# Two attention stages: the first pair's bias, queries and keys loaded in the stage ahead

## The reference

```python
# layer 0, attention part
s = einsum('bthd,bsd->bths', qib, ki) * (D_I ** -0.5)
score = einsum('bth,bths->bts', wb * (H_I ** -0.5), relu(s))
_, idx = top_k(where(adm, score, -inf), 256)
bias = t5_table[_t5_bucket(sel_pos - pb)]
logits = einsum('bthd,btkhd->bhtk', qb, ks) * (DH ** -0.5) + bias
out = einsum('bhtk,btkhd->bthd', softmax(logits), vs)
# layer 1, attention part
rel = clip(q_pos[:, None] - k_pos[None, :], -128, 128) + 128
logits = einsum('bthd,bshd->bhts', q, k) * (DH ** -0.5) + rel_table[rel]
out = einsum('bhts,bshd->bthd', softmax(logits), v)
```

## Time and profile before

| | us |
|---|---|
| median of 3 runs | 3113.55 |
| lowest and highest | 3110.88, 3113.63 |
| the profiled execution | 3111.68 |
| its span in the trace | 3109.8 |
| front stage ends, pa begins | about 580 |
| trunk 0 ends, pc begins | about 2006 |

### The profile page before, as it was taken

One profiled execution on the slowest core, in us unless ns is written; L12 is line 12 of the kernel. 1 busy time (PEld: TensorE's weight loads), 2 busy tenths in 40 slices (PEclk: granted clock), 3 DMA queues, 4 the chain that ended last, 5 costly groups with the idle time before them and its releaser, 6 DMA issues. The chain is left out here.

```text
span 3109.8 us, 60214 instructions
## 1 busy us (share of the span) xinstructions
PE 2917.9 (94%) x25097; PEld 2716.4 (87%) x25097; DVE 1653.1 (53%) x2959; ACT 951.2 (31%) x1984; POOL 1321.6 (42%) x1082
## 2 busy tenths in 40 slices
PE   7999999886789899999999999899889999999998
PEld 5859999664679899999999999766689999999998
DVE  6399999564646644445346400055536644444345
ACT  3341211354433433332101311165524333332001
POOL 2112212373533877776334222100114877775334
PEclk8999999998889999999999999999989999999999
DMA  5816763633241122223321232352121122224222
GB/s 211 256 61 228 235 212 106 180 108 110 99 164 55 49 83 83 82 70 133 102 83 62 81 103 74 95 191 86 64 85 45 66 83 80 71 78 153 83 74 72
DMA packets 160465, 338.82 MB, mean 109 GB/s; under 512 B 21033, under 2 KB 94529, under 8 KB 152193
## 3 DMA queue, kind: packets, MB, share of 16 engines
q1 hardware_dynamic: 119856, 281.64, 27.0%
q10 hardware_dynamic: 40336, 53.31, 4.8%
HBM read 268.30 MB, written 79.49 MB: 112 GB/s over the span
## 5 line engine op out<-in xcount | busy, mean ns | idle before, releaser
L108 PE MATMUL tr_acc<-tr_quad_hi,ah_ring_hi 128*128 128x264 f32 x2432 | 696.3, 286 | 18.8 <-DVE tr_kept L1142 13.2
L110 PE MATMUL tr_acc<-tr_quad_hi,ah_ring_lo 128*128 128x264 f32 x2432 | 694.7, 286 | 0.0
L109 PE MATMUL tr_acc<-tr_quad_lo,ah_ring_hi 128*128 128x264 f32 x2432 | 692.4, 285 | 0.0
L552 POOL TENSOR_TENSOR ah_ring_lo<-ah_raw,ah_ring_hi 128x512 fp32r<-128x512 f32 (+1 forms) x402 | 553.9, 1383 | 183.0 <-ACT ah_ring_hi L889 169.2
L108 PEld LDWEIGHTS tr_acc<-tr_quad_hi,ah_ring_hi 128*128 128x128 f32 x2432 | 461.0, 190 | 19.7 <-DVE tr_kept L1142 13.6
L109 PEld LDWEIGHTS tr_acc<-tr_quad_lo,ah_ring_hi 128*128 128x128 f32 x2432 | 461.2, 190 | 0.1
L110 PEld LDWEIGHTS tr_acc<-tr_quad_hi,ah_ring_lo 128*128 128x128 f32 x2432 | 460.4, 189 | 0.0
L550 POOL CAST ah_ring_hi<-ah_raw 128x512 fp32r<-128x512 f32 (+1 forms) x172 | 113.4, 659 | 592.3 <-PE tr_acc L110 527.2
L108 PE MATMUL tr_acc<-tr_part_hi,ah_ring_hi 128*128 128x352 f32 x1038 | 335.5, 323 | 2.0 <-DVE tr_kept L1191 2.0
L109 PE MATMUL tr_acc<-tr_part_lo,ah_ring_hi 128*128 128x352 f32 x1038 | 332.8, 321 | 0.0
L110 PE MATMUL tr_acc<-tr_part_hi,ah_ring_lo 128*128 128x352 f32 x1038 | 332.5, 320 | 0.0
(11 more groups left out here) (399 smaller groups left out, 6484.6 us busy)
## 6 DMA issues: line engine op xcount, KB each, us to landing
f_ada_w<-in_w_ada_dram SPq DMA_DIRECT2D x48, 1024.0 KB, 5.5
scratch_inner<-tr_kept ACTq DMA_DIRECT2D x88, 264.0 KB, 2.4
tr_staged<-scratch_inner SPq DMA_DIRECT2D x44, 528.0 KB, 4.0
ah_raw<-in_w_gate_dram SPq DMA_DIRECT2D x44, 512.0 KB, 3.5
ah_raw<-in_w_up_dram SPq DMA_DIRECT2D x44, 512.0 KB, 4.5
ah_raw<-in_w_down_dram SPq DMA_DIRECT2D x64, 256.0 KB, 3.1
f_raw<-in_w_dram SPq DMA_DIRECT2D x24, 512.0 KB, 7.4
out_z_dram<-f_stage ACTq DMA_DIRECT2D x60, 176.0 KB, 1.9
```

Source lines behind the costliest of these rows:

```text
L108: pe.matmul(out, w_hi, hi, start=start, stop=False)
L109: pe.matmul(out, w_hi, lo, start=False, stop=False)
L110: return pe.matmul(out, w_lo, hi, start=False, stop=stop)
L552: pool.tensor_tensor(lo[:, 0:width], own, hi[:, 0:width].bitcast(F32), ALU.subtract).then_inc(w_ready, 1)
```

## The change

For each attention stage three of the four loads of pair 0 (bias, queries, keys) are taken out of the stage and issued by SP at the end of the stage ahead, into memory that is dead there and that the attention stage keeps at the same address. The values of pair 0 are still loaded in the attention stage. A class `FirstPair` holds the three tiles and one semaphore. In the front stage SP now waits for the skewed tables, for the last split of the weights and for the stores of all projected chunks, issues the three loads, then stores the mask, then waits for the loads. In trunk 0 SP waits until the stores of the first five units of `z1` (30 of them, ten for each of three semaphores) have landed, issues the loads and waits for them. In the attention stage POOL and PE no longer wait for pair 0, and the counts of later pairs are one lower. Tiles of the attention stage are laid around the kept region, `spread` now ahead of `probT`, and the late sample values of pa take the kept region's place instead of the two bias buffers.

```diff
+            if ahead:
+                for r in range(3):
+                    sp.wait_ge(stored[r], 16 * 2 * 5)
+                ahead.loads(sp)
+                ahead.done(sp)
...
+        ahead = next_pair(m, raw_at)
+        assert ahead.end <= raw_at + 2 * 8 * KD * P
...
+            sp.wait_ge(lines_out, 48)
+            sp.wait_ge(w_ready, len(units))
+            projected = store_no[plan.last_step[len(units) - 3]] + 1
+            for r in range(3):
+                sp.wait_ge(stored[r], 16 * len(range(r, projected, 3)))
+            ahead.loads(sp)
             store_mask(sp)
-            sp.wait_ge(lines_out, 48)
+            ahead.done(sp)
...
+class FirstPair:
+    def __init__(self, m, name, z, q0, k0, skew, width, at):
+        nc = m.nc
+        self.at, self.end = at, at + 8 * width + 8 * T
+        self.bias = nc.alloc_sbuf_tensor_at(f"{name}_bias0", [P, 2, width], F32, offset=at)
+        self.q, self.k = (nc.alloc_sbuf_tensor_at(f"{name}_{x}0", [P, T], F32, offset=at + 8 * width + 4 * T * n)
+                          for n, x in enumerate("qk"))
+        self.sources = (z[q0][:, 0:T], z[k0][:, 0:T], shifted(skew[0:2], P, width + P - 1, P - 1, width))
+        self.landed = m.sem(f"{name}_first")
+    def loads(self, sp):
+        q, k, bias = self.sources
+        sp.dma_start(self.bias[:], bias).then_inc(self.landed, 16)
+        sp.dma_start(self.q[:], q).then_inc(self.landed, 16)
+        sp.dma_start(self.k[:], k).then_inc(self.landed, 16)
+    def done(self, sp):
+        sp.wait_ge(self.landed, 48)
...
-                sp.dma_start(q[b][:], z[q0 + g][:, 0:T]).then_inc(qk_in[b], 16)
-                sp.dma_start(k[b][:], z[k0 + g][:, 0:T]).then_inc(qk_in[b], 16)
+                if g:
+                    sp.dma_start(q[b][:], z[q0 + g][:, 0:T]).then_inc(qk_in[b], 16)
+                    sp.dma_start(k[b][:], z[k0 + g][:, 0:T]).then_inc(qk_in[b], 16)
...
+                if g:
+                    sp.dma_start(bias[b][:], shifted(skew[2 * g:2 * g + 2], P, width + P - 1, P - 1, width)).then_inc(bias_in[b], 16)
...
-                if i == 0:
-                    pool.wait_ge(bias_in[b], 16 * (g // 2 + 1))
+                if i == 0 and g:
+                    pool.wait_ge(bias_in[b], 16 * ((g + 1) // 2))
...
-                if i == 0:
-                    pe.wait_ge(qk_in[b], 32 * (g // 2 + 1))
+                if i == 0 and g:
+                    pe.wait_ge(qk_in[b], 32 * ((g + 1) // 2))
```

More of the change, by code:

```diff
@@ L8 @@
+import math
 from contextlib import ExitStack
@@ L295, in done, with trunk_phase @@
         pool.wait_ge(self.w_lo, AHEAD)
-def trunk_phase(nc, io, l, x, c, places, early):
+def trunk_phase(nc, io, l, x, c, places, early, next_pair=None):
     last = l == 1
@@ L379, in trunk_phase @@
         y_stored = m.sem(f"{name}_y_stored")
+        ahead = next_pair(m, base + 11 * QUAD) if next_pair else None
+        assert ahead is None or ahead.end <= base + 14 * QUAD
         block = m.block()
@@ L1522, in chunk, with front_phase @@
         return self.units[u][1][a] if kind == "z" else None
-def front_phase(nc, io, moving, low_at, score, c):
+def front_phase(nc, io, moving, low_at, score, c, next_pair):
     plan = FrontPlan()
@@ L1532, in front_phase @@
     with Tools(nc) as m:
+        raw_at = nc.sbuf_base
         raw = [m.sb(f"f_raw{b}", [P, 2 * KD * P]) for b in range(2)]
@@ L2065, in __init__, with attention_phase @@
         self.quads = [(lo, min(lo + 4, self.blocks)) for lo in range(0, self.blocks, 4)]
-def attention_phase(nc, name, io, z, q0, k0, vt, v0, skew, width, heads, back, mask, side, ident, mix, early=None, next_weights=None):
+class FirstPair:
[14 more added lines that the diff above has]
+        sp.wait_ge(self.landed, 48)
+def attention_phase(nc, name, io, z, q0, k0, vt, v0, skew, width, heads, back, mask, side, ident, mix, first, early=None, next_weights=None):
     pairs = heads // 2
@@ L2105, in attention_phase, with sb @@
     with Tools(nc) as m:
[L2106 to L2110, removed]
+        def sb(tile, shape):
+            if nc.sbuf_base <= first.at < nc.sbuf_base + 4 * math.prod(shape[1:]):
+                m.sb(f"{name}_kept_free", [P, (first.end - nc.sbuf_base) // 4])
+            return m.sb(tile, shape)
+        q, k = [first.q, sb(f"{name}_q1", [P, T])], [first.k, sb(f"{name}_k1", [P, T])]
+        v = [sb(f"{name}_v{b}", [P, TILES, P]) for b in range(2)]
+        bias = [first.bias, sb(f"{name}_bias1", [P, 2, width])]
+        extra_all = sb(f"{name}_extra", [P, 4, T]) if mask is not None else None
         extra = [extra_all[:, a, :] for a in range(4)] if mask is not None else None
-        prob_all = m.sb(f"{name}_prob", [P, 6 * max(keys)])
+        prob_all = sb(f"{name}_prob", [P, 6 * max(keys)])
         prob = [prob_all[:, max(keys) * a:max(keys) * a + max(keys)] for a in range(6)]
[L2114 to L2117, removed]
+        spread = [sb(f"{name}_spread{b}", [P, 4 * P]) for b in range(2)]
+        probT = [sb(f"{name}_probT{a}", [P, 2 * max(keys)]) for a in range(2)]
+        least, total, inv = (sb(f"{name}_{x}", [P, 2 * U]) for x in ("least", "sum", "inv"))
+        oT = [sb(f"{name}_oT{b}", [P, T]) for b in range(2)]
         dots = [m.ps(f"{name}_dots{a}", [P, 1024]) for a in range(2)]
@@ L2120, in attention_phase @@
         out = [m.ps(f"{name}_out{b}", [P, 512]) for b in range(2)]
-        s_q = m.sb(f"{name}_s_q", [P, G, 4, S])
-        s_k_new, s_v_new = m.sb(f"{name}_s_k_new", [P, 2 * G, S]), m.sb(f"{name}_s_v_new", [S, 256 * G])
+        s_q = sb(f"{name}_s_q", [P, G, 4, S])
+        s_k_new, s_v_new = sb(f"{name}_s_k_new", [P, 2 * G, S]), sb(f"{name}_s_v_new", [S, 256 * G])
         own_sides = G if mask is None else 1
-        s_k = [m.sb(f"{name}_s_k{g}", [P, 2, side.past]) for g in range(own_sides)]
-        s_v = [m.sb(f"{name}_s_v{g}", [P, side.blocks, 256]) for g in range(own_sides)]
+        s_k = [sb(f"{name}_s_k{g}", [P, 2, side.past]) for g in range(own_sides)]
+        s_v = [sb(f"{name}_s_v{g}", [P, side.blocks, 256]) for g in range(own_sides)]
         if mask is not None:
             s_k.append(extra_all[:].rearrange("p (c a) n -> p c (a n)", c=2))
-            s_v.append(bias_all[:].rearrange("p b h n -> p (b h n)").rearrange("p (i n) -> p i n", n=256))
-        s_bias = [m.sb(f"{name}_s_bias{g}", [P, side.keys]) for g in range(G)]
-        s_prob = [] if mask is None else [m.sb(f"{name}_s_prob", [P, side.keys])]
+            s_v.append(nc.alloc_sbuf_tensor_at(f"{name}_s_v{own_sides}", [P, side.blocks, 256], F32, offset=first.at))
+            assert first.end - first.at >= 4 * side.blocks * 256
+        s_bias = [sb(f"{name}_s_bias{g}", [P, side.keys]) for g in range(G)]
+        s_prob = [] if mask is None else [sb(f"{name}_s_prob", [P, side.keys])]
         s_prob += [prob_all[:, side.keys * b:side.keys * b + side.keys] for b in range(2 - len(s_prob))]
         s_mask = s_prob[0]
[L2133 to L2136, removed]
+        s_tail = [sb(f"{name}_s_tail{b}", [S, P]) for b in range(2)]
+        s_least, s_total, s_inv = sb(f"{name}_s_least", [P, G, 4]), sb(f"{name}_s_sum", [P, G]), sb(f"{name}_s_inv", [P, G])
+        s_o = [sb(f"{name}_s_o{b}", [P, DH]) for b in range(2)]
+        s_oT = [sb(f"{name}_s_oT{b}", [DH, P]) for b in range(2)]
         s_small_in = m.sem(f"{name}_s_small_in")
@@ L2166, in loads @@
                     sp.wait_ge(dots_done, TILES * (g - 1))
-                sp.dma_start(q[b][:], z[q0 + g][:, 0:T]).then_inc(qk_in[b], 16)
-                sp.dma_start(k[b][:], z[k0 + g][:, 0:T]).then_inc(qk_in[b], 16)
+                if g:
+                    sp.dma_start(q[b][:], z[q0 + g][:, 0:T]).then_inc(qk_in[b], 16)
+                    sp.dma_start(k[b][:], z[k0 + g][:, 0:T]).then_inc(qk_in[b], 16)
                 if g >= 2:
                     sp.wait_ge(logits, 2 * TILES * (g - 1))
-                sp.dma_start(bias[b][:], shifted(skew[2 * g:2 * g + 2], P, width + P - 1, P - 1, width)).then_inc(bias_in[b], 16)
+                if g:
+                    sp.dma_start(bias[b][:], shifted(skew[2 * g:2 * g + 2], P, width + P - 1, P - 1, width)).then_inc(bias_in[b], 16)
                 if g >= 2:
@@ L3240, in build_program, with first_pair @@
         heads = []
+        firsts = []
+        def first_pair(*of):
+            firsts.append(FirstPair(*of))
+            return firsts[-1]
         def recurrence_head(tools, tensors):
@@ L3250, in build_program @@
                 low_at = nc.sbuf_base + 4 * KD * N
-                front_phase(nc, io, Halves(f, "h00", [P, KD, N]), low_at, score, c)
+                front_phase(nc, io, Halves(f, "h00", [P, KD, N]), low_at, score, c, lambda tools, at: first_pair(
+                    tools, "pa", io["z0"], QA, KA, io["skew_a"], T, at))
             attention_phase(nc, "pa", io, io["z0"], QA, KA, io["zt0"], 0, io["skew_a"], T, HA, None, score,
                             SampleSide(io["ka_past"], io["va_past"], PAST, io["skew_s"], SKEW_S, S - 1, io["mask_s"]),
```

(7 more changed lines are left out.)

## The result

| | before | changed |
|---|---|---|
| median, first comparison (5 runs each) | 3113.63 us | 3097.84 us |
| lowest and highest | 3110.88, 3120.45 | 3096.91, 3102.94 |
| ratio | | 0.9947, 95% interval 0.9931 to 0.9963 |
| profiled span | 3109.8 us | 3095.4 us |

The account below looks back on a forecast made before the run. PE's pace bounds most stages, but load waits bound the starts of pa and pc. Removing 13.57 us, other terms 0, gave 3098.1 from the profiled execution and 3100.0 from the median; forecast 3099.0 us, range 3094 to 3106.

Parts of the forecast that it names:

- What is removed: Starts of pa and pc: waits for pair 0's loads go, gaining 7.32 and 6.25 us, together 13.57 us.
- The bound that ends last: Starts of pa and pc: POOL's clears, 0.46 and 0.67 us, set the new start, ahead of PE and ACT bounds.
- Two signs: Stage starts: POOL uses the bias within 0.8 us of the barrier; DVE's first addition 1.3 us after it in pc.
- The values of pair 0: Still loaded inside pa and pc, now issued first; at most 0.9 and 0.6 us late, cost taken as 0.
- case (C): Rival: late values or pair 2 loads replace a removed wait in one stage; 3103 to 3107 us, chance 0.08.
- Pair 2 of pa: Its bias, wanted at 633.81, lands by about 629.8; cost 0, or 1.6 us if the DMA relief fails.
- What is added ahead: Front stage and trunk 0: moved loads hide behind running work; cost 0, with 1 us kept for each stage.
- the 8.6 us at which the prediction has a store hold PE: Front stage: a store delays PE only beyond about three steps of 2.86 us; at most 9.6 us expected.
- The clock: PE's half clock after the stage starts: term taken as 0; a loss could add 3.56 us busy time per stage.
- a clock that stays up: Rival at the starts of pa and pc: PE keeps 2.4 GHz, up to 5.5 us more gained, chance 0.10.
- the 2 us that the prediction gave as its sign: Both attention stages: time from DVE's first addition to the stage's end stays as before to within 2 us.
- the sum: Whole run: 13.57 us off gives 3098.1 us from the profiled execution, 3100.0 from the median.

Follow-up runs that it names:

- pool_first: Changed kernel with POOL's two clears for the sample tokens moved behind the fourth unit; ratio 0.9938 (0.9926 to 0.9951).
- v_last: Changed kernel with the values of pair 0 issued behind pair 1's four loads; one execution, 3112.51 us, span 3110.7.
- late_loads: Changed kernel with the moved loads issued only after the last stores of the stage ahead have landed; median 3111.58 us, ratio 0.9996.
- warm: Changed kernel with 12 unread matmuls keeping PE busy at the end of the front stage and trunk 0; median 3102.96 us, ratio 0.9968.
- changed-again: The changed kernel itself, unaltered, run once more in more executions; median 3100.1 us, ratio 0.9944 (0.9931 to 0.9958).
- pa_only: Changed kernel with the three loads issued ahead for pa alone, pc loading inside its stage; median 3108.81 us, ratio 0.9980.
- pc_only: Changed kernel with the three loads issued ahead for pc alone, pa loading inside its stage; median 3105.91 us, ratio 0.9976.
- qk_only: Changed kernel with only queries and keys of pair 0 loaded ahead, the bias loaded inside both stages; one execution, 3110.32 us.
- none_ahead: Changed kernel's tiles and layout, but all three loads of pair 0 issued inside both stages again; median 3113.76 us, ratio 0.9999.

## Why the prediction was right

**What is removed: right, at most 0.4 us too large.** Forecast 7.32 + 6.25 = 13.57, measured 7.24 + 5.90 = 13.14. The bound that ends last was POOL's clears in both, as said; pool_first shows it by taking them away. In pc POOL left the barrier 0.31 us after ACT (1999.18 against 1998.88), where in before both left it at 2006.15. That is a matter of the mark: the last stores of trunk 0 in before and in the changed kernel are

```profile
2002.78 0.34 ACTq L962 DMA_DIRECT2D out_zt_dram<-tr_value  x1
```

```profile
1995.80 0.34 ACTq L970 DMA_DIRECT2D out_zt_dram<-tr_value  x1
```

From them POOL's clears follow after 3.37 and 3.38 us, so POOL is not late; the other engines leave the barrier 0.3 us sooner. DVE's first addition follows after 10.89 and 4.70 us, 6.19 gained, and in pa, by the same mark, after 11.27 and 4.03, 7.24 gained. So the removed waits are 13.1 to 13.4 us. Two signs were set too tight in pc: POOL used the bias 1.03 us after the barrier and DVE started 1.63 after it, where 0.8 and 1.3 were given.

**The values of pair 0: right.** They landed 3.9 us after issue in both stages, the lower end of the range, and PE did not wait. The changed kernel's DMA issues (KB each, then us to landing), and the line of its timeline with PE's first use of the values:

```profile
pa_v<-out_zt_dram SPq DMA_DIRECT2D x1, 512.0 KB, 3.9
...
pc_v<-out_zt_dram SPq DMA_DIRECT2D x1, 512.0 KB, 3.9
```

```profile
588.30 0.44 PE L2360 MATMUL pa_out<-pa_probT,pa_v 128*64 128x128 f32 x4
```

Landed at 585.2, wanted at 588.3. v_last shows what case (C) would have cost: 10.2 us of waiting.

**Pair 2 of pa: right.** Its bias was issued at 622.28, landed 8.1 us later at 630.4 and was wanted at 635.09. Between unit 4 and unit 20 DVE's additions keep the same distance to those of before to 0.02 us, so no load came late.

**What is added ahead: right.** The timeline and the DMA issues at the moved loads (front stage; then stores beside them in front, loads and stores in trunk 0):

```profile
534.78 0.37 SPq L2100 DMA_DIRECT2D pa_bias<-scratch_skew_a  x1
...
538.32 0.38 ACT L1896 ACTIVATE f_stage<-f_acc 128x256 f32<-128x256 f32 x1 [2.47 <-PE f_acc L111]
...
568.99 0.33 SPq L1477 DMA_DIRECT2D scratch_mask_s<-score  x1
578.45 0.34 ACTq L1899 DMA_DIRECT2D out_zt_dram<-f_stage  x1
```

```profile
out_zt_dram<-f_stage ACTq DMA_DIRECT2D x1, 128.0 KB, 7.0
...
pc_k<-out_z_dram SPq DMA_DIRECT2D x1, 512.0 KB, 9.1
...
out_zt_dram<-tr_value ACTq DMA_DIRECT2D x2, 128.0 KB, 5.9
```

ACT's step is still 0.38 + 2.47 us. The longest store beside the moved loads took 7.0 us in front and 6.4 in trunk 0 (the row of two has the middle, 5.9), where a store with nothing beside it took 1.8; both are under the 8.6 us at which the prediction has a store hold PE. Nor was anything lost: in front ACT's stores come 1.37 us later than before ahead of the moved loads (533.03 against 531.66) and 1.37 us later at the end (578.45 against 577.08); in trunk 0 they keep their distance to 0.01 us. The mask was stored 34 us after the first load was issued. The Trainium skill, page "DMA: Bandwidth & Descriptors", section "Issuing engines are not separate DMA queues", says that DMAs of all issuing engines run on the same 16 DMA engines and interleave; the longer stores agree with it. What the same bytes cost without cover late_loads shows: 8.1 us, with the mask's store among them, and 6.7.

**The clock: the value 0 held, the bounds were too wide on the side of a gain.** The forecast left up to 3.8 + 1.7 us for a clock that stays up. warm had it stay up in pa and found 0.55 us: the bound took all of PE's half-clock time as if it lay on the path, while in warm the first three units came no sooner than before. On the side of a loss, the first units lost 1.4 to 1.5 us in pa in changed-again, pa_only, pc_only and qk_only, and 1.9 in pc in warm, within the 3.56 us allowed. In changed-again this and a second loss, told next, made the rest of pa 3.9 us longer than before, outside the 2 us that the prediction gave as its sign.

**What the sum left out.** The clock outside the starts. In the first profile the front stage was 1.37 us longer than before long before the first new instruction; and after unit 20 of pa 1.57 us were lost. The stretches by busy time show both, first before and then the changed kernel, each with PEclk as the third number from the end of the row:

```profile
170.00:175.00 5.00, 5.00 (x21) 2.41 (x18) 3.69 (x7) 3.12 (x5) 0.00 (x0) 0.82 0.13 39
...
670.00:675.00 5.00, 3.31 (x26) 2.12 (x28) 3.12 (x10) 2.97 (x6) 4.82 (x3) 1.00 0.00 0
```

```profile
170.00:175.00 5.00, 5.00 (x16) 2.73 (x14) 3.26 (x5) 1.60 (x3) 0.00 (x0) 0.50 0.12 38
...
665.00:670.00 5.00, 4.37 (x18) 2.46 (x18) 1.75 (x5) 1.93 (x6) 4.24 (x3) 0.66 0.01 3
```

In both kernels PE idles 2.9 us at this point of pa while DVE prepares the recurrence. In before the clock held, as in none_ahead, late_loads and warm; in the changed kernel and in seven of the runs, pc_only (whose pa is untouched) among them, it fell, and 1.6 us were lost each time. These are as large as several terms of the sum, with either sign.

**Where the number was helped.** The sum gave 3098.1 from the profiled execution and 3100.0 from the median, and the forecast took the middle. The measured median, 3097.84, is 2.2 us under the sum from the median, so the closeness of 1.2 us is in part luck; the mechanism does not rest on it.

**What stays open.** The ratios, 0.9947 and 0.9944, stand for about 17 us, the traces of the starts for 13.1 to 13.4. Both intervals reach 13.1 us (0.9958), and pa_only and pc_only add up to 13.7. Whether some 3 us more come from a clock that is on average better placed behind the earlier starts was not settled. Each execution has its mean granted clock on record. Among the 31 executions of before that stand beside none_ahead, one with a clock higher by 0.001 was 1.4 us shorter, and in the last series the changed kernel's five average 0.9720 against 0.9692 in the nine of before: by an estimate from these numbers 4 us, the size of what is open. But a higher mean comes in part from the removed waits themselves, in which PE stood idle at half clock, and none_ahead averages 0.9715 against 0.9703 without being faster. So this is a correlation and no cause shown.

## What to carry to other kernels

At the start of a stage, take the first operation in which the engines' work meets (here DVE's first addition), and write down when each of its inputs would be ready without the load, the makers' other first work counted in; the latest of these times is the new start, and the gain is the old start less this one. It is not the time of the loads, and it is not one engine's wait: PE's in pa shrank by 8.41 - 3.36 = 5.05 us where the stage gained 7.2. Half of the tiles brought less than half here. It is worth having where the stage ahead still computes for longer than the loads take and has a dead region of memory; without that cover the same loads cost what they saved. And where the granted clock moves, judge a change of 0.4% by the stretch it touches in each trace, since the rest of the span differs by as much from one execution to the next.

## What the runs showed of the hardware

The three moved loads of pa, 2048 KB, and the mask's store behind them cost 8.1 us with no work to cover them, those of pc, 1664 KB, 6.7 us (late_loads). The values' load of 512 KB in pa took 3.9 us when issued first, 8.0 behind three others (2048 KB), and 10.3 behind pair 1's four loads (2560 KB) in v_last. A 128 KB store took 1.8 us alone and up to 7.0 beside the moved loads. Engines need not leave a barrier together: at the start of pc ACT and SP left it 3.1 us after the last store's issue in the changed kernel and 3.4 us after it in before, POOL 3.4 us after it in both. PE's granted clock can fall after a restart although PE was idle for only 1.35 us before it (warm, pc: 0.60 from 2002 to 2007, 0.50 from 2007 to 2012), and after the same 2.9 us pause in pa it was lower in 8 of the 12 profiled kernels and not in the other 4.
